# Expert blocks of 112 token slots in place of 128

## The chip, the cores and the metric

The kernel runs on one core of a Trainium2 chip. The metric is the device time of one launch in microseconds; shown is the median of several launches. A profile is of one execution, whose own span is a little shorter than the time of a launch.

## The reference, cut to what matters

The program is a two-layer trunk for 320 tokens (256 of a new stream and 64 of a running one). The second layer ends in a top-2-of-8 mixture of expert SwiGLUs; only this part is touched.

```python
D_MODEL, N_EXPERTS, TOP_K, EXPERT_D_FF = 1024, 8, 2, 2816
probs = jax.nn.softmax((x @ router).astype(f32), axis=-1)
top_p, top_e = lax.top_k(probs, TOP_K)
top_p = top_p / jnp.sum(top_p, -1, keepdims=True)
# every token goes through its two experts, weighted by top_p:
#   y[t] = sum over its experts e of  p_e * (silu(x[t] @ w1[e]) * (x[t] @ w3[e])) @ w2[e]
```

All is float32. 320 tokens times two choices are 640 rows for eight experts, 80 on average. Evaluated on the inputs of the runs, the reference's router gives the experts 73, 77, 87, 76, 79, 81, 74 and 93 tokens.

## The kernel before

**Dense part.** The first half of the span is the two mixers, the dense feed-forward and their norms. Its weights come in 1 MB tiles through a ring, and the products have 128 weight columns stationary and 320 tokens moving. The change does not touch it.

**Expert part.** `expert_loops` (on every engine) calls `expert_block` once for expert 0, in a hardware loop for experts 1 to 7, and then for `n_extra` further blocks, one for each expert that has more tokens than one block holds, and more for one with over twice as many. Here the tokens are stationary and the weights move. A block has BLK = 128 token slots: `xe_hi` and `xe_lo` hold its tokens' 1024 features, turned, as 8 operands of 128 features by BLK slots. The 2816 hidden columns are done in three strips of 1024, 1024 and 768 (`WIDTHS`). In `up` (L1238 on), each of the 8 feature groups of a strip takes one "unit" of w1 or w3 (128 rows by the strip's width); each float32 product is three float32r matmuls (`xe_hi` with `w_hi`, `xe_lo` with `w_hi`, `xe_hi` with `w_lo`: L1245 to L1247), over pieces of 512 or 256 moving columns. ScalarE takes the SiLU of one product out of PSUM (L2831), VectorE multiplies it with the other (L2185, into `eg`). `hidden_to_rows` (L1250) turns `eg` in 22 PE transposes a block (L1254): the data is the stationary operand, `ident` the moving one. ScalarE rounds what comes out into `gt_hi` or `gz_hi` (L2837), VectorE keeps the rest in `gt_lo` or `gz_lo` (L2192), and `down` (L1256 on) uses these as stationary operands for w2, 1024 columns wide (L1269 to L1271).

**Which tokens.** `choose` (VectorE) makes `pick_r`, a 0/1 matrix of token by slot; `chosen_rows` (three small matmuls, L1214) makes of it the row number and weight of each slot. GpSimd gathers the next block's tokens with an indirect DMA of one row a slot (`gather`, L2968) into `xg`; `gathered_features` turns them in 8 PE transposes (L1222). `scatter` (L2976) adds the weighted results to `y_rows` in the same way. The first block's tokens are picked by matmuls instead (L1305), and the last block's results go by matmuls (L1322) in place of a scatter. Both lie once in the program.

**Weights.** SyncE loads w1, w3 and w2 in pieces of two units (1 MB or 768 KB) into `moe_ring`, a ring of seven; before each it waits for the slot's old piece to be used (semaphore `e_lo`). ScalarE rounds each unit into `w_hi` (L2787), VectorE subtracts (`w_lo`, L2061); these hold seven units.

**Order.** It is written by hand: each engine's program is a fixed list, tied to the others by semaphores that count units (`e_hi`, `e_lo`, `e_used`) and steps (`e_silu`, `e_g`, `e_gt`, `e_rows`, `e_row`). 8 blocks have 8 x (288 + 132) = 3360 float32r matmuls, 8 x (22 + 8) = 240 transposes.

Of the kernel before, what the change touches and what calls it, by code (L numbers as in the profile page):

```python
# [7 lines left out]
F32R = mybir.dt.float32r  # L8
I32 = mybir.dt.int32
U32 = mybir.dt.uint32  # L10
ALU = mybir.AluOpType
# [43 lines left out]
BLK = 128  # L55
# [20 lines left out]
def mixed_trunk(nc, ins, outs):  # L76
    ctx = ExitStack()
    with ctx:
# [19 lines left out]
        slots = sb("slots", [P, BLK])  # L98
# [32 lines left out]
        gt_words = 2 * (STRIP + WIDTHS[-1])  # L131
# [4 lines left out]
        pick_r = sb("pick_r", [P, 3, BLK], F32R)  # L136
        sb("arena_mid", [P, split_at - PICK0 - 3 * BLK])
# [4 lines left out]
        gt_hi = sb("gt_hi", [P, STRIP], F32R)  # L142
        gt_lo = sb("gt_lo", [P, STRIP], F32R)
        gz_hi = sb("gz_hi", [P, WIDTHS[-1]], F32R)
        gz_lo = sb("gz_lo", [P, WIDTHS[-1]], F32R)
# [162 lines left out]
        e_.take(3 * BLK)  # L308
# [194 lines left out]
        def parts(s):  # L503
            return [(0, 512), (512, WIDTHS[s])]

# [22 lines left out]
        def _(pe):  # L528
# [681 lines left out]
            def chosen_rows(count, b):  # L1210

                pe.wait_ge(S("e_pick"), count)
                for i in range(3):
                    mm = pe.matmul(b[:, 0:4], pick_r[:, i, :], token_row[:, i, :], start=(i == 0), stop=(i == 2))  # L1214
                mm.then_inc(S("e_row_full"), 1)

            def gathered_features(count):

                pe.wait_ge(S("e_gathered"), 16 * (count - 1))
                for half in range(2):  # L1220
                    for k in range(4):
                        mm = pe.transpose(E_T[half][:, k * BLK:(k + 1) * BLK], xg[:, (4 * half + k) * P:(4 * half + k + 1) * P],  # L1222
                                          ident[:, :])
                    mm.then_inc(S("e_features_full"), 1)

            def expert_block(n, e, j_extra):
# [10 lines left out]
                def up(i0, s, banks):  # L1237

                    for k in range(KC):
# [3 lines left out]
                        for (c0, c1), b in zip(parts(s), banks):  # L1243
                            w = c1 - c0
                            pe.matmul(b[:, 0:w], xe_hi[:, k, :], hi_[:, c0:c1], start=(k == 0), stop=False)  # L1245
                            pe.matmul(b[:, 0:w], xe_lo[:, k, :], hi_[:, c0:c1], start=False, stop=False)  # L1246
                            mm = pe.matmul(b[:, 0:w], xe_hi[:, k, :], lo_[:, c0:c1], start=False, stop=(k == KC - 1))  # L1247
                        mm.then_inc(S("e_used"), 1)

                def hidden_to_rows(s):  # L1250
                    pe.wait_ge(S("e_g"), NS * n + s + 1)
                    for (c0, c1), b in zip(parts(s), E_T):
                        for c in range(c0, c1, P):
                            mm = pe.transpose(b[:, c - c0:c - c0 + BLK], eg[:, c:c + P], ident[:, :])  # L1254
                        mm.then_inc(S("e_gt_full"), 1)

                def down(s, rows):
# [3 lines left out]
                    for j in rows:  # L1261
# [5 lines left out]
                        for half in range(2):  # L1267
                            cols = slice(half * 512, (half + 1) * 512)
                            pe.matmul(E_Y[half][:, :], g_hi[:, g], hi_[:, cols], start=first, stop=False)  # L1269
                            pe.matmul(E_Y[half][:, :], g_lo[:, g], hi_[:, cols], start=False, stop=False)  # L1270
                            mm = pe.matmul(E_Y[half][:, :], g_hi[:, g], lo_[:, cols], start=False, stop=final)  # L1271
# [1862 lines left out]
```

## Time and profile before

| | us |
|---|---|
| median of 3 runs | 1475.47 |
| lowest, highest | 1475.02, 1476.70 |
| span of the profiled execution | 1473.8 |

The profile's page gives the busy time of each engine, the span in 40 slices, the DMA queues, the chain of work that ended last and the costliest groups of instructions. PE is the matmul record of TensorE, PEld its weight loads, which run beside matmuls; records of matmuls overlap, so the distance from one start to the next is what one of them costs, not its record's length. DVE is VectorE, ACT ScalarE, POOL GpSimd, SP SyncE.

### The profile page before, as it was taken

Reading aid. Unit: us, or ns where it says so; the run is one execution under the profiler, and the core shown is the slowest. Engines: PE = TensorE matmul, PEld = TensorE weight load, DVE = VectorE, ACT = ScalarE, POOL = GpSimd, SP = SyncE. Lnnn points to the kernel's source line nnn. Section 1 sums busy time; section 2 is a strip of 40 time slices with the busy share of each in tenths; the row PEclk is TensorE's granted clock in tenths of the full one; section 3 lists DMA queues with packets and bytes.
Section 4 is the critical chain, followed back from the end, with each engine's and each line's share of the span. In section 5 each row is a group of like instructions: output and inputs, shape, how many; then the busy total and the mean of one; then the engine's idle time right before and its main releaser. Section 6 shows DMA issues by size and latency. Waiting matters only on the chain.

```text
span 1473.8 us, 29020 instructions
## 1 busy us (share of the span) xinstructions
PE 1439.8 (98%) x11165; PEld 1291.2 (88%) x11166; DVE 1189.5 (81%) x1615; ACT 937.5 (64%) x1238; POOL 74.8 (5%) x151
## 2 busy tenths in 40 slices
PE   8999999999999999999999999999999999999997
PEld 8989988999999899888788888888888888888884
DVE  5687888555445798877998998899989899898997
ACT  4463154533333696475777877788777887877873
POOL 8300000000000000000000000000000000000000
PEclk9999999999999999999999999999999999999999
DMA  9521005445444353216999999999999999999992
GB/s 270 161 88 36 4 3 157 143 148 160 144 143 152 115 158 116 87 58 248 336 389 396 407 397 398 342 398 383 370 397 349 410 379 365 398 343 410 396 350 87
DMA packets 162223, 371.76 MB, mean 252 GB/s; under 512 B 10232, under 2 KB 85968, under 8 KB 162128
## 3 DMA queue, kind: packets, MB, share of 16 engines
q1 hardware_dynamic: 159352, 361.18, 66.7%
q0 software_dynamic: 2160, 7.87, 2.0%
q8 instruction: 69, 1.13, 0.3%
q10 hardware_dynamic: 616, 1.37, 0.2%
q14 instruction: 26, 0.21, 0.0%
HBM read 360.68 MB, written 9.71 MB: 251 GB/s over the span
## 4 chain that ended last, share of the span: by engine, by line
PE 88%; DVE 7%; ACT 3%; issue 1%; ACTq 0%; DVEq 0%
PE bank L1245 11%; PE bank L1246 11%; PE bank L1247 11%; PE bank L556 9%; PE bank L557 9%; PE bank L558 9%; PE bank L1269 5%; PE bank L1271 5%; PE bank L1270 5%; PE bank L656 4%; PE bank L1254 1%; PE bank L1007 1%; DVE wd_lo L1342 1%; PE bank L569 1%; PE bank L573 1%
## 5 line engine op out<-in xcount | busy, mean ns | idle before, releaser
L2061 DVE TENSOR_TENSOR w_lo<-moe_ring,w_hi 128x1024 fp32r<-128x1024 f32 (+1 forms) x560 | 608.5, 1158 | 28.9 <-ACT w_hi L2787 28.9
L2787 ACT ACTIVATE w_hi<-moe_ring 128x1024 fp32r<-128x1024 f32 (+1 forms) x560 | 531.5, 1014 | 70.6 <-PE bank L1271 39.0
L1245 PE MATMUL bank<-w_hi,xe_hi 128*128 128x512 f32 (+1 forms) x768 | 288.4, 376 | 1.6 <-DVE w_lo L2061 1.4
L1246 PE MATMUL bank<-w_hi,xe_lo 128*128 128x512 f32 (+1 forms) x768 | 286.1, 373 | 0.0
L1247 PE MATMUL bank<-w_lo,xe_hi 128*128 128x512 f32 (+1 forms) x768 | 285.6, 372 | 0.0
L1342 DVE TENSOR_TENSOR wd_lo<-arena,wd_hi 128x1024 fp32r<-128x1024 f32 x141 | 169.9, 1209 | 133.3 <-ACT wd_hi L2318 133.0
L556 PE MATMUL bank<-in_hi,wd_hi 128*128 128x320 f32 x800 | 250.9, 314 | 2.4 <-DVE wd_lo L1342 1.2
L558 PE MATMUL bank<-in_hi,wd_lo 128*128 128x320 f32 x800 | 247.5, 309 | 0.0
L557 PE MATMUL bank<-in_lo,wd_hi 128*128 128x320 f32 x800 | 247.5, 309 | 0.0
L2318 ACT ACTIVATE wd_hi<-arena 128x1024 fp32r<-128x1024 f32 (+1 forms) x140 | 146.2, 1047 | 157.3 <-PE bank L558 151.9
L1245 PEld LDWEIGHTS bank<-w_hi,xe_hi 128*128 128x128 f32 x768 | 144.6, 188 | 28.4 <-DVE w_lo L2061 2.9
L1247 PEld LDWEIGHTS bank<-w_lo,xe_hi 128*128 128x128 f32 x768 | 144.3, 188 | 25.7
L1246 PEld LDWEIGHTS bank<-w_hi,xe_lo 128*128 128x128 f32 x768 | 144.6, 188 | 24.8
L556 PEld LDWEIGHTS bank<-in_hi,wd_hi 128*128 128x128 f32 x800 | 150.2, 188 | 5.7 <-issue 1.8
L557 PEld LDWEIGHTS bank<-in_lo,wd_hi 128*128 128x128 f32 x800 | 150.3, 188 | 0.4
L558 PEld LDWEIGHTS bank<-in_hi,wd_lo 128*128 128x128 f32 x800 | 150.2, 188 | 0.0
L1269 PE MATMUL bank<-w_hi,gt_hi 128*128 128x512 f32 x256 | 101.4, 396 | 0.2 <-DVE w_lo L2061 0.2
L1271 PE MATMUL bank<-w_lo,gt_hi 128*128 128x512 f32 x256 | 99.8, 390 | 0.0
L1270 PE MATMUL bank<-w_hi,gt_lo 128*128 128x512 f32 x256 | 99.8, 390 | 0.0
L556 PE MATMUL bank<-hid_hi,wd_hi 128*128 128x320 f32 x224 | 69.8, 312 | 1.3 <-DVE wd_lo L1342 1.3
L558 PE MATMUL bank<-hid_hi,wd_lo 128*128 128x320 f32 x224 | 69.2, 309 | 0.0
L557 PE MATMUL bank<-hid_lo,wd_hi 128*128 128x320 f32 x224 | 69.2, 309 | 0.0
(438 smaller groups left out, 1816.1 us busy)
## 6 DMA issues: line engine op xcount, KB each, us to landing
moe_ring<-in_moe_w SPq DMA_DIRECT2D x216, 1024.0 KB, 8.7
moe_ring<-in_moe_w SPq DMA_DIRECT2D x64, 768.0 KB, 5.6
arena<-in_ffn_w SPq DMA_DIRECT2D x30, 1024.0 KB, 5.3
arena<-in_w_in_c SPq DMA_DIRECT2D x16, 1024.0 KB, 5.3
arena<-in_w_in_ab SPq DMA_DIRECT2D x12, 1024.0 KB, 5.4
arena<-in_w_out_ab SPq DMA_DIRECT2D x4, 1024.0 KB, 5.0
arena<-in_w_out_c SPq DMA_DIRECT2D x4, 1024.0 KB, 5.0
arena<-in_ffn_w SPq DMA_DIRECT2D x4, 768.0 KB, 4.3
```

What stands on the lines that cost most here:

```text
L556: pe.matmul(b[:, 0:T], w_[0][:, cols], x_hi, start=start, stop=False)
L557: pe.matmul(b[:, 0:T], w_[0][:, cols], x_lo, start=False, stop=False)
L558: return pe.matmul(b[:, 0:T], w_[1][:, cols], x_hi, start=False, stop=stop)
L1245: pe.matmul(b[:, 0:w], xe_hi[:, k, :], hi_[:, c0:c1], start=(k == 0), stop=False)
L1246: pe.matmul(b[:, 0:w], xe_lo[:, k, :], hi_[:, c0:c1], start=False, stop=False)
L1247: mm = pe.matmul(b[:, 0:w], xe_hi[:, k, :], lo_[:, c0:c1], start=False, stop=(k == KC - 1))
L1269: pe.matmul(E_Y[half][:, :], g_hi[:, g], hi_[:, cols], start=first, stop=False)
L1270: pe.matmul(E_Y[half][:, :], g_lo[:, g], hi_[:, cols], start=False, stop=False)
L1271: mm = pe.matmul(E_Y[half][:, :], g_hi[:, g], lo_[:, cols], start=False, stop=final)
L1342: dve.tensor_tensor(wd_lo[:, m_ % DENSE_UNITS, 0:words], src, rounded_of(m_)[:, 0:words], ALU.subtract).then_inc(S("dense_lo"), 1)
L2061: dve.tensor_tensor(w_lo[:, i % UNITS, 0:unit_words(i)], moe_unit(i), w_hi[:, i % UNITS, 0:unit_words(i)], ALU.subtract)\
L2787: act.activation(w_hi[:, i % UNITS, 0:unit_words(i)], moe_unit(i), ACT.Copy).then_inc(S("e_hi"), 1)
```

## The change

BLK becomes 112. Buffers that stay 128 wide for other uses (`slots`, `pick_r`) are given P = 128 instead. A block's operands become 112 slots wide: `xe_hi`, `xe_lo` and each 128-column group of `gt_*`, `gz_*` (addressed through the new function `turned`). Instructions on rows of slots have 112 partitions. An expert with over 112 tokens (before: over 128) takes a further block.

```diff
-BLK = 128
+BLK = 112
...
+        def turned(c0, c1):
+
+            return slice(c0 // P * BLK, c1 // P * BLK)
...
-                    mm = pe.matmul(b[:, 0:4], pick_r[:, i, :], token_row[:, i, :], start=(i == 0), stop=(i == 2))
+                    mm = pe.matmul(b[0:BLK, 0:4], pick_r[:, i, 0:BLK], token_row[:, i, :], start=(i == 0), stop=(i == 2))
...
-                        mm = pe.transpose(E_T[half][:, k * BLK:(k + 1) * BLK], xg[:, (4 * half + k) * P:(4 * half + k + 1) * P],
-                                          ident[:, :])
+                        mm = pe.transpose(E_T[half][:, k * BLK:(k + 1) * BLK], xg[0:BLK, (4 * half + k) * P:(4 * half + k + 1) * P],
+                                          ident[0:BLK, 0:BLK])
...
-                            pe.matmul(b[:, 0:w], xe_hi[:, k, :], hi_[:, c0:c1], start=(k == 0), stop=False)
-                            pe.matmul(b[:, 0:w], xe_lo[:, k, :], hi_[:, c0:c1], start=False, stop=False)
-                            mm = pe.matmul(b[:, 0:w], xe_hi[:, k, :], lo_[:, c0:c1], start=False, stop=(k == KC - 1))
+                            pe.matmul(b[0:BLK, 0:w], xe_hi[:, k, :], hi_[:, c0:c1], start=(k == 0), stop=False)
+                            pe.matmul(b[0:BLK, 0:w], xe_lo[:, k, :], hi_[:, c0:c1], start=False, stop=False)
+                            mm = pe.matmul(b[0:BLK, 0:w], xe_hi[:, k, :], lo_[:, c0:c1], start=False, stop=(k == KC - 1))
...
-                            mm = pe.transpose(b[:, c - c0:c - c0 + BLK], eg[:, c:c + P], ident[:, :])
+                            mm = pe.transpose(b[:, turned(c - c0, c - c0 + P)], eg[0:BLK, c:c + P], ident[0:BLK, 0:BLK])
...
-                            pe.matmul(E_Y[half][:, :], g_hi[:, g], hi_[:, cols], start=first, stop=False)
+                            pe.matmul(E_Y[half][0:BLK, :], g_hi[:, g], hi_[:, cols], start=first, stop=False)
...
-                    dve.tensor_tensor(xe_lo[:, 4 * half:4 * half + 4, :], E_T[half][:, :].rearrange("p (k n) -> p k n", k=4),
+                    dve.tensor_tensor(xe_lo[:, 4 * half:4 * half + 4, :], E_T[half][:, 0:4 * BLK].rearrange("p (k n) -> p k n", k=4),
...
-                        ins_ = dve.tensor_tensor(eg[:, c0:c1], eh[:, c0:c1], E_H3[h][:, 0:c1 - c0], ALU.mult)
+                        ins_ = dve.tensor_tensor(eg[0:BLK, c0:c1], eh[0:BLK, c0:c1], E_H3[h][0:BLK, 0:c1 - c0], ALU.mult)
...
-                        act.activation(dst[:, c0:c1], E_T[h][:, 0:c1 - c0], ACT.Copy).then_inc(S("e_gt_hi"), 1)
+                        act.activation(dst[:, turned(c0, c1)], E_T[h][:, turned(0, c1 - c0)], ACT.Copy).then_inc(S("e_gt_hi"), 1)
...
-                pool.indirect_dma_start(xg[:, :], None, x_rows[:, :], bass.IndirectOffsetOnAxis(ap=x_row[:, 0:1], axis=0))\
+                pool.indirect_dma_start(xg[0:BLK, :], None, x_rows[:, :], bass.IndirectOffsetOnAxis(ap=x_row[0:BLK, 0:1], axis=0))\
```

The same cut to 112 is made in the other matmuls of `down`, in the first block's pick (L1305), the scatter, the row and weight columns, and the last block's rows (L1322).

No instruction is added, removed or moved on any engine. TensorE at the second strip's transposes, before and then changed (the shape is output partitions by moving columns; `arena` in the transposes is `eg`):

```order
L1247 MATMUL bank<-w_lo,xe_hi 128x512
L1245 MATMUL bank<-w_hi,xe_hi 128x512
L1246 MATMUL bank<-w_hi,xe_lo 128x512
L1247 MATMUL bank<-w_lo,xe_hi 128x512
L1254 MATMUL bank<-ident,arena 128x128 x8
L1245 MATMUL bank<-w_hi,xe_hi 128x512
```

TensorE at the same place of the changed kernel:

```order
L1251 MATMUL bank<-w_lo,xe_hi 112x512
L1249 MATMUL bank<-w_hi,xe_hi 112x512
L1250 MATMUL bank<-w_hi,xe_lo 112x512
L1251 MATMUL bank<-w_lo,xe_hi 112x512
L1258 MATMUL bank<-ident,arena 128x112 x8
L1249 MATMUL bank<-w_hi,xe_hi 112x512
```

The order is the same; float32r products keep their 512 moving columns and have 112 output rows, the eight transposes keep 128 stationary columns and have 112 moving ones.

## Rows read from the trace of the kernel before

**Rows 1.** Windows of the expert part: busy us, instructions, granted clock, DMA share, GB/s.
```profile
core 0: us, PE busy (x) PEld busy (x) DVE busy (x) ACT busy (x) POOL busy (x), PEclk, DMA share, GB/s
...
800.00:900.00 100.00, 100.00 (x482) 84.12 (x481) 90.91 (x101) 79.91 (x93) 4.84 (x5) 1.00 1.02 395
...
1300.00:1400.00 100.00, 100.00 (x483) 84.19 (x482) 89.60 (x107) 80.00 (x95) 4.10 (x4) 1.00 0.99 380
```

**Rows 2.** Waits of TensorE from 700 to 1454 us: total, times, longest us.
```profile
PE bank L1245 <- DVE w_lo L2061: 1.4, 3, 0.7
PE bank L1245 <- DVE xe_lo L2242: 0.2, 1, 0.2
PE bank L1269 <- DVE w_lo L2061: 0.2, 1, 0.2
```

**Rows 3.** Timeline of TensorE: start us, length us; first strip, 512 columns each.
```profile
812.18 0.39 PE L1245 MATMUL bank<-w_hi,xe_hi 128*128 128x512 f32 x1
...
814.90 0.39 PE L1245 MATMUL bank<-w_hi,xe_hi 128*128 128x512 f32 x1
```

**Rows 4.** Timeline of TensorE: third strip, 512 and 256 columns in turn.
```profile
1045.90 0.40 PE L1245 MATMUL bank<-w_hi,xe_hi 128*128 128x512 f32 x1
...
1046.60 0.28 PE L1245 MATMUL bank<-w_hi,xe_hi 128*128 128x256 f32 x1
...
1046.95 0.40 PE L1245 MATMUL bank<-w_hi,xe_hi 128*128 128x512 f32 x1
```

**Rows 5.** Timelines of TensorE: a block's transposes, two earlier turns, the slots' row numbers.
```profile
1049.05 1.03 PE L1254 MATMUL bank<-ident,arena 128*128 128x128 f32 x8
1049.84 0.47 PE L1245 MATMUL bank<-w_hi,xe_hi 128*128 128x512 f32 x1
...
153.07 2.40 PE L691 MATMUL bank<-ident,arena 128*64 128x128 f32 x40
...
566.66 1.43 PE L1007 MATMUL bank<-arena 128*64 128x64 f32 x40
...
699.31 0.47 PE L1214 MATMUL bank<-token_row,pick_r 128*128 128x4 f32 x3
```

**Rows 6.** Groups by line and shape, PE and its loads: count, busy us, mean ns.
```profile
L1246 PEld LDWEIGHTS bank<-w_hi,xe_lo 128*128 128x128 f32 x768 | 144.6, 188 | 24.8
L1053 PEld LDWEIGHTS bank<-arena 64*128 64x128 f32 x80 | 4.8, 188 | 2.5 <-issue 1.5 <-DVE arena L1930 0.9
L1254 PEld LDWEIGHTS bank<-ident,arena 128*128 128x128 f32 x176 | 20.3, 140 | 2.1
L1007 PEld LDWEIGHTS bank<-arena 128*64 128x64 f32 x560 | 18.1, 138 | 1.1 <-DVE arena L1930 0.4 <-issue 0.4
L691 PEld LDWEIGHTS bank<-ident,arena 128*64 128x64 f32 x40 | 2.2, 137 | 0.1
L1170 PEld LDWEIGHTS bank<-arena,logit_w 128*32 128x32 f32 x22 | 0.7, 109 | 0.8 <-issue 0.3
...
L1254 PE MATMUL bank<-ident,arena 128*128 128x128 f32 x176 | 23.1, 272 | 0.0
L1222 PE MATMUL bank<-ident,arena 128*128 128x128 f32 x64 | 8.3, 272 | 0.0
```

**Rows 7.** Waits of SyncE's queue over the span, and of ScalarE from 700 us.
```profile
SPq L3078 <- DVE w_lo L2061: 586.0, 272, 9.2
...
ACT w_hi L2787 <- DMA moe_ring<-in_moe_w: 3.8, 7, 0.9
```

**Rows 8.** The chain of work before the first expert product: start us, length us.
```profile
694.80 4.33 DVE w_lo L2061 x4
699.25 0.69 DVE xe_lo L2242
699.99 0.50 PE bank L1245
```

**Rows 9.** The chain of work after the last expert product.
```profile
1454.50 0.24 PE bank L1271
1454.76 0.69 ACT arena L2820
1455.50 1.14 PE bank L1322 x2
```

More of the change, by code:

```diff
@@ L97, in mixed_trunk @@
         reset = sb("reset", [P, T])
-        slots = sb("slots", [P, BLK])
+        slots = sb("slots", [P, P])
         row_number = sb("row_number", [P, 3, 1])
@@ L141, in mixed_trunk @@
         xe_lo = sb("xe_lo", [P, KC, BLK], F32R)
[L142 to L145, printed above, removed]
+        gt_hi = sb("gt_hi", [P, STRIP // P * BLK], F32R)
+        gt_lo = sb("gt_lo", [P, STRIP // P * BLK], F32R)
+        gz_hi = sb("gz_hi", [P, WIDTHS[-1] // P * BLK], F32R)
+        gz_lo = sb("gz_lo", [P, WIDTHS[-1] // P * BLK], F32R)
         moe_ring = sb("moe_ring", [P, MOE_RING, TILE])
@@ L307, in mixed_trunk @@
         assert e_.at == PICK0
-        e_.take(3 * BLK)
+        e_.take(3 * P)
         pick = pick_r.bitcast(F32)
@@ L1268, in down @@
                             cols = slice(half * 512, (half + 1) * 512)
[L1269 to L1271 removed]
+                            pe.matmul(E_Y[half][0:BLK, :], g_hi[:, g], hi_[:, cols], start=first, stop=False)
+                            pe.matmul(E_Y[half][0:BLK, :], g_lo[:, g], hi_[:, cols], start=False, stop=False)
+                            mm = pe.matmul(E_Y[half][0:BLK, :], g_hi[:, g], lo_[:, cols], start=False, stop=final)
                         mm.then_inc(S("e_used"), 1)
@@ L1304, in _ @@
                     for i in range(3):
-                        mm = pe.matmul(E_T[half][:, k * BLK:(k + 1) * BLK], xtok[:, i, f], pick[:, i, :], start=(i == 0), stop=(i == 2))
+                        mm = pe.matmul(E_T[half][:, k * BLK:(k + 1) * BLK], xtok[:, i, f], pick[:, i, 0:BLK], start=(i == 0), stop=(i == 2))
                 mm.then_inc(S("e_features_full"), 1)
@@ L1321, in last_rows @@
                             pe.wait_ge(S("e_y"), 2 * n - 1 + half)
-                        pe.matmul((E_H1, E_H3, E_T)[i][half][0:rows, :], pick[:, i, 0:rows], ey[:, half * 512:(half + 1) * 512],
+                        pe.matmul((E_H1, E_H3, E_T)[i][half][0:rows, :], pick[0:BLK, i, 0:rows], ey[0:BLK, half * 512:(half + 1) * 512],
                                   start=(i == 0), stop=True).then_inc(S("y_normal"), 1)
@@ L2241, in _ @@
                 dve.wait_ge(S("e_rows_hi"), half + 1)
-                dve.tensor_tensor(xe_lo[:, 4 * half:4 * half + 4, :], xg[:, half * 512:(half + 1) * 512].rearrange("p (k n) -> p k n", k=4),
+                dve.tensor_tensor(xe_lo[:, 4 * half:4 * half + 4, :], xg[:, 4 * half * BLK:4 * (half + 1) * BLK].rearrange("p (k n) -> p k n", k=4),
                                   xe_hi[:, 4 * half:4 * half + 4, :], ALU.subtract).then_inc(S("e_rows"), 1)
@@ L2811, in features_rounded @@
                     act.wait_ge(S("e_features_full"), 2 * count - 1 + half)
-                    act.activation(xe_hi[:, 4 * half:4 * half + 4, :], E_T[half][:, :].rearrange("p (k n) -> p k n", k=4),
+                    act.activation(xe_hi[:, 4 * half:4 * half + 4, :], E_T[half][:, 0:4 * BLK].rearrange("p (k n) -> p k n", k=4),
                                    ACT.Copy).then_inc(S("e_rows_hi"), 1)
```

42 lines of the change are left out of this document (21 added, 21 removed).

## The prediction, made before the changed kernel was run

> **What bounds the kernel now.** The first view to read is the table of windows. From 700 us on the expert part is the same in every window: TensorE busy for all of it, at a granted clock of 1.00, VectorE about 90%, ScalarE about 80% [rows 1]. A busy TensorE is not yet a bound, so the second view is its waits: from 700 to 1454 us they come to 1.8 us, the longest of them 0.7 us [rows 2]. So the expert part lasts as long as TensorE's own list of instructions, start to start. ScalarE and VectorE are behind it, not ahead: what they save is worth nothing unless it is one of those 1.8 us. The dense part, before 700 us, holds nothing that the change touches.
>
> The third view is the timeline, for what one instruction costs there. In a first strip thirteen starts lie between 812.18 and 814.90, twelve steps of 227 ns for 512 moving columns [rows 3]. In a third strip the three 512-column matmuls take 0.70 us and the three of 256 columns 0.35 us, 117 ns each [rows 4]. From 256 to 512 columns the step goes from 117 to 227 ns: it follows the moving columns, almost in proportion. Every matmul has a new stationary operand, whose load is recorded at 188 ns but runs beside the matmul before it [rows 6].
>
> **The float32r products.** 3360 of them, some 720 us (2976 x 0.227 + 384 x 0.117), and the change narrows only their stationary operand and the rows of their output. The moving columns, the weights, are the same in number, and these set the step. I cost them at nothing. The cover is the step itself: a load has 227 ns (512 columns) or 117 ns (256) to be done in. The load of 128 columns alone can be bounded: the three tiny matmuls of L1214 move only 4 columns and still take (0.47 - 0.25) / 2 = 0.11 us each, which must be their loads of 128 columns [rows 5] (0.25 us is the record of one). So a load takes about 110 ns of the 117 that a 256-column step gives. It just fits; and there may be a little lost: six matmuls of a third strip take 1.05 us, where 3 x 227 for the 512s and half as much for the 256s plus their share of the fixed part (227 against 213 ns for 512 columns at the granted 2.4 GHz, 14 ns; so 107 + 14 = 121 ns) would be 1.04 us. 0.01 us times 128 such sixes (8 feature groups, two products, 8 blocks) is 1.2 us at the very most that shorter loads could give back; rounding in the rows is of the same size, so I take 0.4 us, and keep 0 and 1.2.
>
> **The transposes.** 22 + 8 a block, 176 and 64 in all [rows 6]; they stand in TensorE's list between products, so they count in full. Eight of them have a record of 1.03 us, one of 0.27: (1.03 - 0.27) / 7 = 109 ns a step [rows 5]. They keep 128 stationary columns (the data), and their moving operand, `ident`, goes from 128 to 112 columns. Is the step set by the moving columns or by the load? Two groups with the same 128x64 stationary operand and the same load (137 and 138 ns, rows 6) tell: 40 of L691 with 128 moving columns take 2.40 us, 40 of L1007 with 64 take 1.43 [rows 5]. They run in pairs, side by side in the array; a pair is 2 x (2.40 - 0.27) / 39 = 109 ns against 2 x (1.43 - 0.22) / 39 = 62 ns. Double the columns, and the step is 1.76 times as long at the same load: moving columns set it, 0.73 ns each by this slope and 109 / 128 = 0.85 by proportion. 16 columns fewer give 12 to 13.6 ns; I take 13. 240 x 13 = 3.1 us. The two ends are 0 (the load sets it) and 240 x 13.6 = 3.3 us.
>
> Here the Trainium skill speaks against the change. "TensorE: Matmul & The Clock Gate", section "LDWEIGHTS (loading the stationary operand)", gives the load's time as its columns over 1.2 GHz, whatever the contraction rows: 107 ns for 128 columns, an estimate by that page, which fits the 109 ns step as well as the moving columns do. By it the transposes would gain nothing, since their 128 stationary columns stay, and the sum would be 0.7 us in place of 3.8. The rows are against it: the load of a transpose is recorded at 140 ns, 48 less than the 188 of a product's operand with as many columns, and about as long as the 137 to 138 ns of a load of 64 columns [rows 6]. I go by the rows, and keep the rule as a rival.
>
> **The slots' row numbers.** Three L1214 matmuls a block, bound by their load as above; 112 of 128 columns save 110 / 8 = 14 ns on two steps and 8 blocks, 0.2 us.
>
> **The two ends of the expert part.** The first product waits for four `w_lo` and then for `xe_lo` [rows 8]; `xe_lo` goes from 512 to 448 elements, 0.08 of its 0.69 us at most. I take 0.1 us with what else is shorter there. The pick matmuls L1305 and the features' scaling lie beside the `w_lo` chain. At the end, the outputs (L2820) and the last rows (L1322) keep 512 elements or moving columns on fewer partitions or contraction rows [rows 9]: nothing.
>
> **What is off the path.** ScalarE's `gt_hi`, `xe_hi` and VectorE's `gt_lo`, `xe_lo` shrink by an eighth; the SiLU and the product into `eg` have fewer partitions and the same elements in a row, so no change. All of that lies behind TensorE. Gather and scatter move 112 rows of 4 KB in place of 128, beside a stream of weights that is a hundred times as large. No queue has an instruction more, and nobody waits for anything new.
>
> **The sum.** 3.1 + 0.4 + 0.2 + 0.1 = 3.8 us less: 1473.8 - 3.8 = 1470.0 us for the span. The median of the runs is 1.7 us above the span (1475.47 against 1473.8), which gives **1471.7 us**, 0.26% less. With the ends of the terms (240 x 12 ns = 2.9 us and 0.3 for the two small ones, against 3.3 + 1.2 + 0.4) this case runs from 1470.6 to 1472.3.
>
> **The rivals.**
>
> *A: the transposes' step is their load.* Then 3.1 us go from the sum: 1475.47 - 0.7 = 1474.8 us. For it: 109 ns is also close to the 110 ns of a load of 128 columns at L1214. Against it: the shorter load record and the pairs above. Chance 0.13.
>
> *B: the weights' stream becomes the bound.* The DMA engines are shown busy for all of the time, at 380 to 395 GB/s [rows 1]. If they can give no more, the time cannot shrink: 1475.2 us. Against it: before nearly each of its 280 pieces SyncE waits for a slot of the ring that VectorE must free, 586 us in all, and ScalarE waits for a piece only 3.8 us in 7 places [rows 7], and never makes TensorE wait by it. The gain asks for 0.5% more bytes a second. Chance 0.05.
>
> *C: the fixed part of a product shrinks with the stationary columns.* The step of 227 ns is 14 ns over 512 columns at 2.4 GHz. If that were something done for each stationary column, 112 of them would save 14 / 8 = 1.7 ns on 3360 products, 5.8 us more: 1465.9 us. For it: no row explains the 14 ns. Against it: nothing in the trace scales with the load while the load is covered. No row has a float32r operand of fewer than 128 columns, so this stays open. Chance 0.10.
>
> *D, the other side: a load of 112 columns is slower than one of 128.* All 3360 float32r loads before have a full 128 columns, so a special path for full operands would not be seen as one. If a narrower load took twice as long, 2 x 97 = 194 ns, it would still hide under a 227 ns step, but not under the 117 ns of the 384 matmuls with 256 columns: 384 x (194 - 117) = 29.6 us, so 1471.7 + 29.6 = 1501 us. It decides from a load time of 117 ns upwards, and from 227 ns all products pay. Against it: loads of 64 and 32 columns are recorded at 138 and 109 ns, shorter the narrower [rows 6], and the full float32r load takes the 188 ns of the full float32 load at L1053. Chance 0.05. The same page of the Trainium skill, section "Weight-path perf modes", says that the fast weight load is on when the operand has 128 weights and is not FP32, and this change would lose it. By these rows there is no fast mode to lose: the float32r load is as long as the float32 one.
>
> *E: a further block.* An expert with 113 to 128 tokens would now take a second block, 3360 / 8 = 420 products, about 91 us: some 1563 us. The fullest expert of these inputs has 93 tokens and the margin is 19, so the change's own branch is never taken. Chance 0.01.
>
> **How the numbers follow.** The forecast has 0.66, A 0.13, B 0.05, C 0.10, D 0.05, E 0.01. A measurement of this kernel tells about 0.2% from no change, which is 2.95 us; the forecast of 3.8 lies only 0.8 beyond that, so of its 0.66 I count 0.53 as faster and 0.13 as within. Faster: 0.53 + 0.10 = 0.63. Within 0.2%: 0.13 + 0.13 + 0.05 = 0.31. Slower: 0.06. The range reaches down to C and up to A and B, with half a microsecond for the median's own scatter: 1465.5 to 1475.9, which leaves out D and E and little else.
>
> **What would show it.** A step of the transposes of 95 to 97 ns (eight in about 0.93 us) in place of 109; a step of 227 ns for 512 columns, unchanged, against 225 under C; a load record of about 174 ns, 14 less than 188, for the products, and 140 still for the transposes; six matmuls of a third strip at 1.04 to 1.05 us; 176 and 64 transposes, so eight blocks; no new waits of TensorE. The prediction is wrong in its main term if the transposes stay at 109 ns, and in its largest zero if the 227 ns moves either way: one nanosecond there is 3.4 us.

## The result, and the profile after

| | before | after |
|---|---|---|
| median, us | 1476.14 (6 runs, 1475.02 to 1478.34) | 1481.54 (6 runs, 1480.07 to 1482.86) |
| span of the profiled execution, us | 1473.8 | 1479.8 |

The changed kernel is slower: the ratio is 1.0035, with a 95% interval of 1.0025 to 1.0046. The forecast was 1471.7 us, with a range up to 1475.9 us, so it has the wrong sign, and the time lies outside the range.

First the lines of the page of after: the span, and the busy time of each engine in us with its share and its instructions.

```profile
span 1479.8 us, 29020 instructions
PE 1446.3 (98%) x11165; PEld 1248.9 (84%) x11166; DVE 1186.4 (80%) x1615; ACT 935.4 (63%) x1238; POOL 78.9 (5%) x151
```

Then the windows of after that answer to [rows 1], and TensorE's waits from 700 to 1460 us, which answer to [rows 2].

```profile
800.00:900.00 100.00, 100.00 (x477) 77.66 (x476) 89.47 (x100) 79.09 (x93) 5.37 (x5) 1.00 1.02 395
1300.00:1400.00 100.00, 100.00 (x483) 77.83 (x482) 88.46 (x99) 75.51 (x90) 3.97 (x4) 1.00 1.00 375
```

```profile
PE bank L1249 <- DVE w_lo L2065: 1.1, 2, 0.7
```

Still busy for all of the time, at a granted clock of 1.00, and with 1.1 us of waits in 760. So no engine and no transfer has come in front of TensorE: its own list takes longer, with the same instructions in it. Which of them? The next lines are the groups of after by line and shape (count, busy us, mean ns of a record, idle before), which answer to [rows 6]. L1250 loads a product's operand; L1258 and L1226 are the two kinds of transposes.

```profile
L1250 PEld LDWEIGHTS bank<-w_hi,xe_lo 128*112 128x112 f32 x768 | 134.1, 175 | 36.0
L1258 PEld LDWEIGHTS bank<-ident,arena 112*128 112x128 f32 x176 | 18.9, 140 | 2.3
L1258 PE MATMUL bank<-ident,arena 112*128 112x112 f32 x176 | 20.8, 258 | 0.0
L1226 PE MATMUL bank<-ident,arena 112*128 112x112 f32 x64 | 7.4, 258 | 0.0
```

The counts are those of before, so there are still eight blocks. The product's load has gone from 188 to 175 ns, the load of a transpose is unchanged. What remains is the distance between starts. These lines are TensorE's timeline in a first strip of after (start us, length us); from the first line to the third are 48 steps.

```profile
892.61 0.39 PE L1249 MATMUL bank<-w_hi,xe_hi 128*112 128x512 f32 x1
892.84 0.39 PE L1250 MATMUL bank<-w_hi,xe_lo 128*112 128x512 f32 x1
...
903.71 0.39 PE L1249 MATMUL bank<-w_hi,xe_hi 128*112 128x512 f32 x1
...
925.66 0.39 PE L1251 MATMUL bank<-w_lo,xe_hi 128*112 128x512 f32 x1
925.89 0.93 PE L1258 MATMUL bank<-ident,arena 112*128 112x112 f32 x8
926.59 0.46 PE L1249 MATMUL bank<-w_hi,xe_hi 128*112 128x512 f32 x1
```

From 892.61 to 903.71 is 11.10 us, or 231 ns a product of 512 moving columns, where [rows 3] have 227. Eight transposes have a record of 0.93 us against 1.03 in [rows 5]: (0.93 - 0.26) / 7 = 96 ns a step, 13 less than before, as predicted.

How much is that in a block? The transposes of the gathered features (L1222 before, L1226 after) come eight times in each of eight blocks, so their first and last start are seven blocks and seven transposes (0.8 and 0.7 us) apart. The lines give the load's shortest, median and longest record in ns and those two starts in us, of before and then of after.

```profile
L1222 PEld LDWEIGHTS bank<-ident,arena x64: 137/139/144, 776.5 to 1434.6; 128*128 128x128 f32 x64
```

```profile
L1226 PEld LDWEIGHTS bank<-ident,arena x64: 137/141/143, 777.1 to 1440.3; 112*128 112x128 f32 x64
```

A block took (658.1 - 0.8) / 7 = 93.9 us and takes (663.2 - 0.7) / 7 = 94.6 us, 0.74 more. Its 30 transposes give back 30 x 0.013 = 0.39 and its row numbers 0.03, so its 420 products cost 0.74 + 0.42 = 1.16 us more, 2.8 ns each. That holds for the second to the eighth block. The first one took 97.22 us and takes 96.97, 0.25 less, so its products cost only 0.17 us more. In all, 7 x 1.16 + 0.17 = 8.3 us are lost on the products and 3.1 + 0.2 gained, which makes 5.0; from the first product's start to the last one's the traces have 754.34 and 759.27 us, 4.9 more. (The first product also starts 1.0 us later in this execution, 700.99 against 699.99 us. Over the profiles of all whole kernels here that start lies anywhere between 699.5 and 701.9 us, and at 701.10 in e3 below, which has the instructions of before; so this microsecond says nothing about the change.)

### The profile page after: what moved, and what is told of

Read it like the earlier page. It is cut to its first block, busy times and chain, and to the rows that moved or that the text cites. A ratio compares the mean times of both kernels' runs of the same rounds, so it can differ in the third digit from the quotient of the medians.

```text
span 1479.8 us, 29020 instructions
## 1 busy us (share of the span) xinstructions
PE 1446.3 (98%) x11165; PEld 1248.9 (84%) x11166; DVE 1186.4 (80%) x1615; ACT 935.4 (63%) x1238; POOL 78.9 (5%) x151
## 4 chain that ended last, share of the span: by engine, by line
PE 89%; DVE 7%; ACT 2%; issue 1%; DMA 0%; SPq 0%; DVEq 0%; ACTq 0%
PE bank L1249 11%; PE bank L1250 11%; PE bank L1251 11%; PE bank L560 9%; PE bank L561 9%; PE bank L562 9%; PE bank L1273 6%; PE bank L1275 6%; PE bank L1274 5%; PE bank L660 4%; PE bank L1258 1%; PE bank L1011 1%; DVE wd_lo L1346 1%; PE bank L573 1%; PE bank L577 1%
## 5 line engine op out<-in xcount | busy, mean ns | idle before, releaser
L1249 PE MATMUL bank<-w_hi,xe_hi 128*112 128x512 f32 (+1 forms) x768 | 288.6, 376 | 1.1 <-DVE w_lo L2065 1.1
L1251 PE MATMUL bank<-w_lo,xe_hi 128*112 128x512 f32 (+1 forms) x768 | 287.6, 375 | 0.0
L1250 PE MATMUL bank<-w_hi,xe_lo 128*112 128x512 f32 (+1 forms) x768 | 287.5, 374 | 0.0
L1249 PEld LDWEIGHTS bank<-w_hi,xe_hi 128*112 128x112 f32 x768 | 134.0, 175 | 38.1 <-DVE w_lo L2065 2.5
L1250 PEld LDWEIGHTS bank<-w_hi,xe_lo 128*112 128x112 f32 x768 | 134.1, 175 | 36.0
L1251 PEld LDWEIGHTS bank<-w_lo,xe_hi 128*112 128x112 f32 x768 | 133.9, 174 | 35.2
L1273 PE MATMUL bank<-w_hi,gt_hi 128*112 128x512 f32 x256 | 101.6, 397 | 0.0
L1275 PE MATMUL bank<-w_lo,gt_hi 128*112 128x512 f32 x256 | 100.4, 392 | 0.0
L1274 PE MATMUL bank<-w_hi,gt_lo 128*112 128x512 f32 x256 | 100.1, 391 | 0.0
```

The lines of the kernel that those rows point to most:

```text
L1249: pe.matmul(b[0:BLK, 0:w], xe_hi[:, k, :], hi_[:, c0:c1], start=(k == 0), stop=False)
L1250: pe.matmul(b[0:BLK, 0:w], xe_lo[:, k, :], hi_[:, c0:c1], start=False, stop=False)
L1251: mm = pe.matmul(b[0:BLK, 0:w], xe_hi[:, k, :], lo_[:, c0:c1], start=False, stop=(k == KC - 1))
L1273: pe.matmul(E_Y[half][0:BLK, :], g_hi[:, g], hi_[:, cols], start=first, stop=False)
L1274: pe.matmul(E_Y[half][0:BLK, :], g_lo[:, g], hi_[:, cols], start=False, stop=False)
L1275: mm = pe.matmul(E_Y[half][0:BLK, :], g_hi[:, g], lo_[:, cols], start=False, stop=final)
```

## The experiments

The question is why a product with the same 512 moving columns takes 231 ns once its stationary operand has 112 columns. A second look at after's timeline narrows it: within a strip the step depends on the feature group k, in a pattern that repeats every four groups. The operand of group k begins k x 448 bytes behind the first one (112 x 4 bytes, where before it was 512). So besides the width, the change also moved where each operand begins relative to the moving rows. And the group alone doesn't settle the step. These are the first product of group k = 3 and that of the group after it, six steps on, in the first strip (with w1) and in the second (with w3) of one block:

```profile
896.77 0.39 PE L1249 MATMUL bank<-w_hi,xe_hi 128*112 128x512 f32 x1
...
898.16 0.39 PE L1249 MATMUL bank<-w_hi,xe_hi 128*112 128x512 f32 x1
...
930.80 0.39 PE L1249 MATMUL bank<-w_hi,xe_hi 128*112 128x512 f32 x1
...
932.16 0.39 PE L1249 MATMUL bank<-w_hi,xe_hi 128*112 128x512 f32 x1
```

That is 231.7 ns a step in the one and 226.7, the step of before, in the other, with the same stationary operands at the same place relative to the moving rows. In the first block, the first strip has 226.5 ns there too. That made two theories, later joined by a third:

- *Width* (W in the expectations): fewer than 128 stationary columns cost some ns a product.
- *Start* (S; SW is both together): the distance in bytes between the operand's start and the moving rows' start decides, in some period.
- *History* (H): equal matmuls in a row settle into one of several steady steps, and what ran before chooses which. Full operands at the start of before always fall back into the shortest one.

"Distance" below is the start of the stationary operand relative to the moving rows', modulo 512 bytes, where before has 0. The mean steps of the whole kernels are taken over stretches in which only products of 512 columns follow each other; they leave out the third strips and the product right behind a group of transposes.

**Width and start apart, in the kernel.** Four kernels, each with one of the two.

e1: 112 slots, each operand still 512 bytes from the next.

```diff
-        xe_hi = sb("xe_hi", [P, KC, BLK], F32R)
+        xe_hi = sb("xe_hi", [P, KC, 128], F32R)
-                            pe.matmul(b[0:BLK, 0:w], xe_hi[:, k, :], hi_[:, c0:c1], start=(k == 0), stop=False)
+                            pe.matmul(b[0:BLK, 0:w], xe_hi[:, k, 0:BLK], hi_[:, c0:c1], start=(k == 0), stop=False)
```

(and the same for `xe_lo`, the `gt` and `gz` tiles and the other matmuls)

> The changed kernel (112 slots) with one thing undone: each stationary operand of 112 columns lies in a 128-column place of its own (a stride of 512 bytes in place of 448), so that every operand starts where it does in the kernel before, and the moving weights lie where they did. Theory S (the operands' start addresses cost the 3 to 4 ns a step): steps of 512 columns back at 227 ns, loads still 175 ns, transposes still 96 ns, and the time 3 to 4 us below the kernel before, about 1472 us. Theory W (112 columns or 112 output rows cost it by themselves): steps stay at 230 to 231 ns and the time at about 1481 us.

e2: 128 slots as before, each operand 576 bytes from the next.

```diff
-BLK = 112
+BLK = 128
-        xe_hi = sb("xe_hi", [P, KC, BLK], F32R)
+        xe_hi = sb("xe_hi", [P, KC, 144], F32R)
```

> 128 slots as in the kernel before, but the stationary operands lie 144 columns apart (576 bytes), so that their starts go through four places within 256 bytes, as in the changed kernel, at full width. Theory S: steps of 512 columns at 229 to 232 ns with a pattern of four over the feature groups, and 8 to 12 us above the kernel before, since nothing is saved on transposes: about 1486 us. Theory W: 227 ns and the time of before, 1476 us.

e3: 128 slots, 512 bytes apart, but `w_hi`, `w_lo` and all operands moved by 256 bytes, as they are by the change (a control).

```diff
+        sb("pad", [P, 64])
         moe_ring = sb("moe_ring", [P, MOE_RING, TILE])
```

> 128 slots and operands 512 bytes apart as in the kernel before, with all of the weights' buffers and stationary operands moved down by 256 bytes, as far within 512 bytes as the changed kernel moved them. Theory S, and theory W: no change, 227 ns and 1476 us. Theory M (what matters is where the moving weights start): 230 ns and 8 to 10 us more.

e4: as e1, with `BLK = 96`.

> Blocks of 96 slots (the fullest expert has 93 tokens, so still eight blocks), each operand in a 128-column place. Theory S: steps at 227 ns, transposes at 96 x 2 / 2.4 + 2 = 82 ns, so 27 ns less than in the kernel before on each of 240: about 6.5 to 7.5 us below it, 1469 us. Theory W: steps above 227 ns again, and the time at or above that of the kernel before.

| | median us | ratio to before (95%) | mean step, 512 columns | us a block |
|---|---|---|---|---|
| before | | | 226.9 ns | 93.91 |
| after | 1481.54 | 1.0035 (1.0025 to 1.0046) | 230.6 | 94.65 |
| e1 | 1483.31 | 1.0044 (1.003 to 1.0058) | 231.6 | 94.86 |
| e2 | 1489.76 | 1.0091 (1.0076 to 1.0106) | 231.7 | 95.59 |
| e3 | 1476.89 | 1.0003 (0.9994 to 1.0012) | 226.9 | 93.91 |
| e4 | 1477.02 | 1.0004 (0.9995 to 1.0013) | 230.0 | 93.93 |

e2 refutes width as the only cause: with full operands the step rises just as much once their distance varies. e1 refutes start as the only cause: with every distance at 0, the narrow operands take no less than after's. e3 shows that moving the weights and the operands together by 256 bytes changes nothing. e4 seems to be no slower than before only because its transposes of 96 columns take 82.6 ns: 240 x (109 - 82.6) = 6.3 us given back. And e1 has something that neither theory holds. This is its timeline around the transposes that stand between the products with w1 and with w3 of the second strip:

```profile
926.07 0.40 PE L1250 MATMUL bank<-w_hi,xe_hi 128*112 128x512 f32 x1
...
926.54 0.40 PE L1252 MATMUL bank<-w_lo,xe_hi 128*112 128x512 f32 x1
926.77 0.93 PE L1259 MATMUL bank<-ident,arena 112*128 112x112 f32 x8
927.47 0.46 PE L1250 MATMUL bank<-w_hi,xe_hi 128*112 128x512 f32 x1
```

Ahead of the transposes all products with w1 of that strip run at 233.3 ns; behind them, the products with w3 and the first strip's with w2 run at 228.8 ns. The operands, their widths and distances are the same on both sides. From w1 to w3 of the first strip, with no transposes between them, nothing changes; but that strip runs at 228.8 ns in the first block and at 233.3 in the seven others.

**TensorE alone.** e5 runs nothing but float32r matmuls, 24 of each kind in a row: 67 kinds with various widths, distances and moving columns, on data that is loaded once. Nearly all of its kinds use one operand and one set of moving rows 24 times. e8 has two of each in turn, as the kernels have, and sweeps the distance in steps of 16 bytes (32 for 128 columns). Of e5, e8 and e12 there is one execution each. The edit shows e8's pattern, where D is the distance in words and W the width:

```diff
+            for i in range(24): pe.matmul(bank[i // 3 % 2][0:W, 0:512], st[:, D + 1024 * (i % 3 % 2):D + 1024 * (i % 3 % 2) + W],
+                                          mv[:, 1024 * (i % 3 // 2) + 512 * (i // 3 % 2):1024 * (i % 3 // 2) + 512 * (i // 3 % 2) + 512],
+                                          start=(i % 3 == 0), stop=(i % 3 == 2))
```

> Nothing of the model is computed: the outputs are zeros, and TensorE alone runs 24 float32r matmuls in a row for each of 67 cases, with ScalarE, VectorE and DMA idle. The cases: 13 widths of the stationary operand from 128 to 64 columns; starts of the operand 16 to 448 bytes further on, for 128, 112 and 96 columns; starts of the moving operand 64 to 256 bytes further on; 256 and 320 moving columns; two operands in turn at the distances used in the kernels. Theory SW (the load's length and its start both enter the step, inside TensorE's own reads): 128 columns at distance 0 give 227 ns, and widths and starts give other steps in the same order as in the kernels, 112 columns at about 231 to 233, 96 at 230. Theory N (the longer step comes from other engines' traffic in the same memory): all 512-column cases give 227 ns or less here.

> TensorE alone again, nothing of the model computed (outputs are zeros), now in the kernels' own pattern: two stationary operands in turn (first, second, first) and the moving rows hi, hi, lo, 24 matmuls for each case. The operand's start goes through 512 bytes in steps of 16, for 112 columns upwards and again downwards, for 96 columns, and in steps of 32 for 128. Theory SW (width and start relative to the moving rows decide the step): 128 columns at distance 0 and 256 give 227 ns and other starts more; 112 columns give 229 to 232 at 0 and 227 at some starts, 320 bytes among them; upward and downward passes agree. If they don't agree, the step depends also on what ran before (a phase between two streams), and 320 bytes need not give 227.

Of e5's timeline, the kinds at distance 0 with 128, 120, 112 and 96 columns (24 matmuls a line; the step is (length - 0.39) / 23):

```profile
27.29 5.60 PE L126 MATMUL bank<-mv,st 128*128 128x512 f32 x24
...
38.17 5.76 PE L128 MATMUL bank<-mv,st 128*120 128x512 f32 x24
...
49.37 5.67 PE L130 MATMUL bank<-mv,st 128*112 128x512 f32 x24
...
71.49 5.68 PE L134 MATMUL bank<-mv,st 128*96 128x512 f32 x24
```

By the starts of the last 13 matmuls of a kind, its settled step: 226.7 ns for 128 columns, 233.3 for 120, 228.8 for 112, 230.0 for 96. No other engine runs beside them, and the DMA engines move about 1 GB/s, so the effect needs TensorE alone. It isn't monotonic in the width either: 124 columns take 226.7, 100, 88 and 80 take 233.3, 64 take 230.0. With full operands, distances of 16, 32 and 64 bytes give 233.3, 128 gives 232.4, 192 gives 228.9, and 256 is again 226.7. Moving the moving operand by m bytes does the same as moving the stationary one by -m within 1 ns in 11 of the 12 kinds that try it; the twelfth, 96 columns at 128 bytes, has 231.7 one way and 226.7 the other. With 256 moving columns and distance 0 narrow is a little faster (128 columns 120.0 ns, 112 columns 117.8, 96 columns 115.8), but there too the start enters: at 64 bytes it is 117.8, 120.0 and 113.3.

And of e8's, with 112 columns at distances 0, 16, 160 and 256:

```profile
29.23 5.66 PE L126 MATMUL bank<-mv,st 128*112 128x512 f32 x24
34.73 5.76 PE L127 MATMUL bank<-mv,st 128*112 128x512 f32 x24
...
84.63 5.60 PE L136 MATMUL bank<-mv,st 128*112 128x512 f32 x24
...
117.49 5.66 PE L142 MATMUL bank<-mv,st 128*112 128x512 f32 x24
```

That is 228.8, 233.3, 226.7 and 228.8 ns: a period of 256 bytes, passed up and down with the same values, and 226.7 at 112, 160, 176 and 208 bytes. But e5, with its one operand in place of two, had 226.7 for 112 columns at 320 bytes, where e8 has 231.7 and where e5 itself has 231.7 at 64 bytes, the same distance in a period of 256; and in e8, 96 columns at 16 bytes take 226.7, and 233.3 at 272 bytes. One kind of matmul, two steps: again something that is neither width nor start.

**Can a better start save the narrow operands?** Three kernels try it: e9 with 112 columns at 320 bytes (e5's fast place), e10 at 160 bytes (e8's fast place), e11 with 96 columns at 16 bytes.

```diff
+        sb("pad2", [P, 80])
         xe_hi = sb("xe_hi", [P, KC, 128], F32R)
```

(e9; `[P, 40]` in e10; in e11 `xe_hi[:, k, 4:4 + BLK]` in place of a pad)

> The changed kernel with its 112-column operands 512 bytes apart, as in the aligned run, but all of them 320 bytes further on relative to the weights, the start at which 112 columns took 226.6 ns with TensorE alone. Theory SW: 227 ns steps with narrow operands and the time of the wide ones, about 1473 us. If the step depends on the phase that other matmuls leave, it can be anything from 227 to 233, and the time 1473 to 1483 us.

> The changed kernel with its 112-column operands 512 bytes apart and 160 bytes further on relative to the weights, a start at which 112 columns take 226.7 ns a step with TensorE alone, upwards and downwards, and whose neighbour at 176 bytes does so too. If width and start relative to the moving rows decide the step (theory SW), the steps are 227 ns with narrow operands, no wait is new, and the time is 3 us below the kernel before, about 1473 us, as with the full operands, where the same operands at 0 bytes gave 1483 us and at 320 bytes 1486 us. If narrow operands cost something of their own, 230 ns or more and 1480 us or more.

> Blocks of 96 slots with narrow operands 512 bytes apart, as in the aligned run of 96 (230.0 ns a step, 1477.0 us), with one thing moved: each operand starts 16 bytes further on in its place, where 96 columns take 226.7 ns with TensorE alone (230.0 at 0). Theory SW: steps of 227 ns, 3.3 ns x 3000 = 9 us off 1477 where all of them follow, but the third strips' short steps need not: 1468 to 1471 us. If the start does not matter inside the kernel: 230 ns and 1477 us.

| | median us | ratio to before (95%) | mean step, 512 columns |
|---|---|---|---|
| e9 | 1486.09 | 1.0064 (1.0051 to 1.0078) | 231.7 ns |
| e10 | 1483.34 | 1.0038 (1.0026 to 1.0049) | 231.4 |
| e11 | 1485.51 | 1.0057 (1.0044 to 1.007) | nearly all 233.3 |

All three miss the hoped-for 227 ns. e9 has the step that e8 measured at its distance. e10 and e11 have places where e8 had 226.7, and run at 233.3 in most strips. The timeline of e10 shows how it comes and goes:

```profile
922.76 0.39 PE L1252 MATMUL bank<-w_hi,xe_hi 128*112 128x512 f32 x1
...
926.26 0.39 PE L1252 MATMUL bank<-w_hi,xe_hi 128*112 128x512 f32 x1
...
926.97 0.93 PE L1261 MATMUL bank<-ident,arena 112*128 112x112 f32 x8
...
928.44 0.39 PE L1252 MATMUL bank<-w_hi,xe_hi 128*112 128x512 f32 x1
...
930.48 0.39 PE L1252 MATMUL bank<-w_hi,xe_hi 128*112 128x512 f32 x1
```

15 steps from 922.76 to 926.26 are 233.3 ns each; then the transposes; then 9 steps from 928.44 to 930.48 are 226.7 each. That lasts for w3 of this strip and the first strip's products with w2; in the next stretch of 512-column products, behind the third strip and its transposes, it is 233.3 again. The kernel's executions also differ more from each other: nine lie between 1477.27 and 1484.77 us, where fourteen of before beside them lie between 1475.68 and 1477.47; that their steps differ from one execution to the next is likely, but only one was profiled.

**History by itself.** e12, again TensorE alone, puts one odd matmul of n moving columns (n from 128 to 308 in steps of 12) ahead of 30 equal ones.

```diff
+            pe.matmul(bank[2][0:128, 0:n], st[:, 0:128], mv[:, 0:n], start=True, stop=True)
+            for i in range(30): pe.matmul(bank[i // 3 % 2][0:W, 0:512], st[:, D + ...
```

> TensorE alone, nothing of the model computed (outputs are zeros): 30 matmuls of 512 columns for each case in the kernels' pattern of two operands in turn, and ahead of each case one odd matmul of 128 columns stationary and n moving columns, n from 128 to 308 in steps of 12. Four cases of width and start: 128 columns at 0, 112 at 0, 112 at 160 bytes, 96 at 16 bytes. Theory H (the step is one of several steady ones, and what ran before chooses among them): 128 columns at 0 come to 226.7 ns whatever n is; 112 at 160 bytes stay at 226.7 ns for some n and at 233.3 for others, 112 at 0 at 228.8 or 233.3, 96 at 16 bytes at 226.7 or 233.3, the pairs that the kernels show. Theory SW as it was (width and start alone): every n ends at 226.7, 228.8, 226.7 and 226.7 ns, and the kernels' other values come from the other engines.

Of its timeline, a line for 30 matmuls each: a full operand at distance 0 (L147), 112 columns at 0 behind n = 176 (L167), then 112 columns at 160 bytes behind n = 212, 224 and 236, then 96 columns at 16 bytes behind n = 200.

```profile
98.53 6.98 PE L147 MATMUL bank<-mv,st 128*128 128x512 f32 x30
...
168.17 7.18 PE L167 MATMUL bank<-mv,st 128*112 128x512 f32 x30
...
301.15 6.97 PE L205 MATMUL bank<-mv,st 128*112 128x512 f32 x30
308.06 7.15 PE L207 MATMUL bank<-mv,st 128*112 128x512 f32 x30
315.15 6.96 PE L209 MATMUL bank<-mv,st 128*112 128x512 f32 x30
...
406.56 6.96 PE L235 MATMUL bank<-mv,st 128*96 128x512 f32 x30
```

The same 30 matmuls take 6.97, 7.15 and 6.96 us when the one ahead of them has 212, 224 and 236 columns. In all:

| operand | behind 16 different n, the settled step is |
|---|---|
| 128 columns, distance 0 | 226.7 ns, always (after at most 10 steps, about 232 ns each but for the first) |
| 112 columns, distance 0 | 228.8 or 228.9 for 15 of them, 233.3 for n = 176 |
| 112 columns, distance 160 | 226.7 for 6 of them, 232 to 233.3 for 10 |
| 96 columns, distance 16 | 226.7 for 5 of them, 233.3 for 11 |

So history is shown: the same instructions settle into one step or another by what ran ahead, and keep it for as long as they were repeated. The small matmul is enough to decide it: behind n = 212 and n = 224 the 30 matmuls before it had both settled at 226.7 ns, and what follows has 226.7 and 233.3. Width and distance decide which steps are seen for an operand. Of the four kinds tried in this way, only the full operand at distance 0 falls back into 226.7 whatever came before. A narrow operand also means fewer output rows; every run changes the two together, so nothing here tells the reading of the one from the writing of the other.

**The gain without the loss.** If this is right, the transposes' gain can be kept by giving the products their full operands back. e6 has 112 slots everywhere, but the operands are 128 columns wide and read in full; the 16 spare columns are filled once and their output rows are never read. e7 is the same with 96 slots.

```diff
+        xe_hi = sb("xe_hi", [P, KC, 128], F32R)
-                            pe.matmul(b[0:BLK, 0:w], xe_hi[:, k, :], hi_[:, c0:c1], start=(k == 0), stop=False)
+                            pe.matmul(b[:, 0:w], xe_hi[:, k, :], hi_[:, c0:c1], start=(k == 0), stop=False)
```

> The changed kernel's 112 slots in the gather, the transposes, the SiLU, the splits and the scatter, but each product reads its full 128-column operand (a stride of 512 bytes, the last 16 columns filled once with finite numbers whose results nobody reads). This is the change without the narrower stationary operand. Theory SW: steps at 227 ns, transposes at 96 ns, about 3 us below the kernel before: 1473 us. If something else in the change costs the time (the writes, fewer partitions on ScalarE and VectorE, the row DMAs), the time stays at 1480 us or more.

> The same with 96 slots: full 128-column operands in the products, 96-wide transposes, gathers and scatters; the fullest expert has 93 tokens, so eight blocks. Theory SW: steps at 227 ns, transposes at 82 to 83 ns, 26 ns x 240 = 6.3 us below the kernel before: 1470 us, faster than both kernels.

| | median us | ratio to before (95%) | step, 512 columns | transposes | us a block |
|---|---|---|---|---|---|
| e6 | 1473.68 | 0.9983 (0.9974 to 0.9992) | 227.0 ns | 95.9 ns | 93.61 |
| e7 | 1472.65 | 0.9978 (0.9968 to 0.9987) | 227.0 | 82.6 | 93.21 |

Both are faster than before, by 0.17% and 0.22%, and both intervals lie below 1. The line of the gathered features' transposes, of e6 and then of e7, shows the shorter blocks: (656.0 - 0.7) / 7 = 93.6 us and (653.1 - 0.6) / 7 = 93.2 us, against 93.9 before.

```profile
L1227 PEld LDWEIGHTS bank<-ident,arena x64: 137/140/143, 777.0 to 1433.0; 112*128 112x128 f32 x64
```

```profile
L1227 PEld LDWEIGHTS bank<-ident,arena x64: 138/140/143, 778.6 to 1431.7; 96*128 96x128 f32 x64
```

e7 gains 0.70 us a block, 5.6 in eight, but only 3.0 us in the span: its first block is 1.3 us longer than before's (98.55 against 97.22 us), where e6's is 0.3 shorter. With 96 slots the bound on blocks an expert may need goes up (T / BLK, rounded up, is 4), so the list of further blocks has more entries for VectorE to go through, just when TensorE waits for the first weights. First the two waits for `w_lo` in e7's waits of TensorE (total, times, longest us), then one of VectorE's steps on that list:

```profile
PE bank L1250 <- DVE w_lo L2065: 1.8, 4, 0.7
PE bank L1273 <- DVE w_lo L2065: 1.3, 1, 1.3
```

```profile
701.33 0.76 DVE L2116 TENSOR_TENSOR arena<-cand,slots 128x576 f32<-128x576 f32 x1
```

Before, that step has 256 elements and takes 0.42 us. That the longer list is what delays `w_lo` fits the times (e4 has 96 slots too, and its first block is 4.5 us longer than its others, where e1's is 2.0), but no run took it away by itself. e7 also pays only while every expert has at most 96 tokens (here the fullest has 93).

## Why the prediction was wrong

**What bounds the kernel**: right. TensorE is busy for all but 1.1 us of the expert part.

**The products, costed at nothing**: this is the step that failed. It read the 227 ns as set by the moving columns, with the load hidden beside them, and concluded that a narrower operand changes nothing. The load is hidden indeed, and did shrink (188 to 175 ns), and twice the columns do take about twice the time. But 227 ns was not the time of 512 moving columns at 2.4 GHz, which is 213.3 ns; it was that and 13.3 ns more, and nothing in the rows said what the 13.3 ns hung on. e5, e8 and e12 show that it isn't fixed: it is most often 13.3, 15.5, 16.7 or 20 ns in steady state, by the operand's width and start and by what ran ahead. Over 3360 products the mean rose by 2.5 ns, and the term put at nothing measures 8.3 us. A sign of it stood in the prediction's own rows: [rows 4] has 0.70 us for three products of 512 columns, 233 ns each and not 227, with the full operands of before, between products of 256 columns. The prediction quotes the 0.70 us, then reckons with 227, and looks for the remainder in the load. The prediction had named this zero as its largest, at 3.4 us a nanosecond. It let one cause move it downwards (rival C); upwards, only a load of over 227 ns would have done it (in rival D). A term with that much under it and an unexplained remainder of 14 ns in it should have had a rival each way. (Two small slips move nothing: 0.01 us times 128 is 1.3 us and not 1.2, and rival B's 1475.2 us has no working, where no gain at all would be 1475.5.)

**The transposes**: right. 109 ns before, 95.9 with 112 moving columns and 82.6 with 96: in proportion to the columns, 0.85 to 0.86 ns each. Their 3.1 us are in after, where the product behind a group of transposes gets shorter as well (299 ns in place of 314). e6 shows them alone, and there that product stays at 314 to 319 ns: the four groups of a block have 26 steps between their 30 transposes, 0.34 us, and with the row numbers' 0.03 and about 0.06 lost on the products its blocks are 0.30 us shorter. From the first product's start to the last one's e6 takes 2.4 us less than before (751.89 against 754.34); its median is 2.6 less. The Trainium skill's rule for loads ("TensorE: Matmul & The Clock Gate", section "LDWEIGHTS (loading the stationary operand)"), by which a load of 128 columns alone takes about 107 ns, has the trace of the transposes against it: with 128 stationary columns still, they went to 82.6 ns in e4 and e7.

**256 moving columns** (0.4 us): not seen. In the kernels their step is 117.6 ns before and 117.7 after, and six products of a third strip take 1.049 us and then 1.048, which is under 0.2 us in all 128 of them. The gain for narrow operands that e5 has at distance 0 comes with the start of before only: e1, which keeps it, has 115.8 ns.

**The slots' row numbers** (0.2 us): right, and for the reason given. The three take 0.25 us up to the next product's start before (946.42 to 946.67) and 0.22 after (948.68 to 948.90), 112 ns and then 98 for each of the two steps, in proportion to the stationary columns. **The start of the expert part** (0.1 us): too small to tell, beside a start that moves by over two microseconds.

**The rivals.** A (load-bound transposes) falls with the 95.9 ns. B (the DMA as the bound) falls with e6 and e7, which ask for weights faster than before and get them. C (a fixed part that shrinks with the stationary columns) had the right suspect and the wrong sign: that part does depend on the operand, but 124 columns leave it, 120 raise it by 6.6 ns and 112 by 2.1 (e5). D (the narrow load is slower) comes out on the side that D was for, by another mechanism: the load became shorter (98 ns in place of 112 where it sets the step, at the row numbers), and the loss is in the 512-column steps that D held safe up to a load of 227 ns. E: there is no further block.

**By what would show it**: transposes at 95 to 97 ns, a load of 174, six matmuls of a third strip at 1.04 to 1.05 us, 176 and 64 transposes, no new waits all came as written. The one that did not is the unchanged 227 ns, which was also named as the one that would break the sum.

## What to carry to other kernels

When a long list of equal instructions sets the time, compare their step with what their columns account for, and treat the remainder as open both ways: a nanosecond is worth as much as the list is long. Narrowing the stationary operand of float32r matmuls saved nothing here at 512 moving columns, and could cost 1 to 3% of each; keep it 128 columns wide and each one 512 bytes from the next even where fewer columns are used (filled once, output unread), and take the narrower size where it pays, in the moving columns of the transposes. A layout that measures fast in an isolated loop may not be fast in the kernel (e10, e11): try it behind several different predecessors.

## What the runs showed of the hardware

- **A float32r matmul of 512 moving columns has several steady steps.** 226.7, 228.8, 230.0 and 233.3 ns are the ones most seen, at a granted clock of 1.00; at 2.4 GHz that is 544, 549, 552 and 560 cycles for 512 columns. It stays in one for a whole strip, and what runs ahead can bring it into another: one small matmul does in e12, and in e1 and e10 it changes across eight transposes. Full operands at distance 0 settle at 226.7 ns only where 512-column products follow each other; between products of 256 columns theirs take 232 ns on average (before, third strips).
- **Where the stationary operand begins relative to the moving rows enters the step.** In e8 it repeats every 256 bytes for 112 and 128 columns, though not for 96 (226.7 and 233.3 ns at 16 and 272 bytes); to move both by 256 bytes changes nothing (e3), and no other engine is needed for it (e5). That the reads of the two operands get in each other's way would fit a period in bytes and a lock-in, but nothing here looks at that: it is argued, not shown, and why 124 columns behave like 128 and 120 don't stays open with it.
- **The fixed part is larger than the Trainium skill has it.** "TensorE: Matmul & The Clock Gate", section "Wait — 56ns, not 53.3ns?", gives a start to start of N / 2.4 GHz and about 2.5 ns, 215.7 ns for 512 columns; here no settled float32r step of 512 columns, each with a load of its own, was under 226.6.
- **float32 transposes fit two cycles a moving column**: 109, 95.9 and 82.6 ns for 128, 112 and 96, each within 3 ns of 2 x columns / 2.4 GHz, with 128 stationary columns in all three. The tiny float32r matmuls of the row numbers go by their stationary columns instead: 112 ns for 128 and 98 for 112.
